# A mixture-of-experts gather: every fourth up row of the first tile summed on VectorE instead of TensorE

## What is computed

```
# x_c: 128 tokens of the normalised stream; 8 heads, top 16 experts of each
s1, s2 = queries . sub-keys;  v1, i1 = top_k(s1, 16);  v2, i2 = top_k(s2, 16)
top_s, pos = top_k(v1[:, None] + v2[None, :], 16);  eidx = i1 * 128 + i2 at pos
g = softmax(top_s)
a = gelu(x_c . expert_down[eidx])              # one number for each token and expert
y = sum over heads and experts of (g * a) * expert_up[eidx]
x = x + y;  out = rmsnorm(x)
```

## Time and profile before

| | |
|---|---|
| median of 3 runs | 1003.92 us (1002.21 to 1005.22) |
| profiled execution | 1000.79 us, span 999.0 us |
| mean granted TensorE clock | 0.938 of full speed |
| first gather issued | 312.15 us from the span's start |
| first dot of tile 0, of tile 1 | 319.87 us, 666.38 us |
| last dot | 988.66 us |
| busy: TensorE, VectorE, ScalarE, GpSimd | 847.4, 563.1, 416.7, 244.0 us |
| moved by the gathers | 268.45 MB, 65.9% of what 16 DMA engines can take in the span |

### The profile page before, as it was taken

One profiled execution on the slowest core, in us unless ns is written; L12 is line 12 of the kernel. 1 busy time (PEld: TensorE's weight loads), 2 busy tenths in 40 slices (PEclk: granted clock), 3 DMA queues, 4 the chain that ended last, 5 costly groups with the idle time before them and its releaser, 6 DMA issues.

```text
span 999.0 us, 9382 instructions
## 1 busy us (share of the span) xinstructions
PE 847.4 (85%) x3163; PEld 478.0 (48%) x3163; DVE 563.1 (56%) x1336; ACT 416.7 (42%) x1082; POOL 244.0 (24%) x267
## 2 busy tenths in 40 slices
PE   5999999999797988988879999887686877877876
PEld 4999986647745635533334355432232322322322
DVE  5544432112225757477686675758668587685743
ACT  5434434213302454356643543435354344343533
POOL 0000000000002332333333423333333333434330
PEclk9999995585998999999999999999999999999999
DMA  9869652000016998999999999999999999999995
GB/s 335 289 144 382 225 212 63 22 0 1 1 41 266 367 406 311 372 423 423 420 415 403 364 423 366 360 423 378 420 421 422 421 420 422 409 407 418 416 422 237
DMA packets 63299, 316.33 MB, mean 317 GB/s; under 512 B 7891, under 2 KB 10004, under 8 KB 30484
## 3 DMA queue, kind: packets, MB, share of 16 engines
q0 software_dynamic: 36864, 268.45, 65.9%
q1 hardware_dynamic: 26340, 47.28, 14.1%
q10 hardware_dynamic: 48, 0.01, 0.0%
HBM read 313.10 MB, written 2.62 MB: 316 GB/s over the span
## 4 chain that ended last, share of the span: by engine, by line
PE 48%; DMA 27%; DVE 15%; ACT 7%; issue 2%; POOL 0%; POOLq 0%; DVEq 0%; ACTq 0%
DMA qkvb<-in_expert_rows,expert_idx 20%; PE y L1152 10%; PE a_bank L964 8%; DMA spare<-in_expert_rows,expert_idx 7%; PE v_bank L1152 7%; PE a_bank L957 6%; PE v_bank L957 6%; DVE qkvb L890 5%; PE v_bank L964 4%; PE v_bank L1043 2%; PE y L1064 2%; DVE spare L890 2%; PE v_bank L1047 1%; ACT diag L617 1%; DVE key_idx L828 1%
## 5 line engine op out<-in xcount | busy, mean ns | idle before, releaser
L462 POOL DMA_INDIRECT qkvb<-in_expert_rows,expert_idx x172 | 162.1, 943 | 592.3 <-DVE expert_idx L866 309.7
L1152 PE MATMUL v_bank<-qkvb,diag 128*128 128x512 f32 x344 | 169.4, 627 | 48.7 <-ACT diag L617 48.7
L610 ACT ACTIVATE gelu<-dots 128x1 f32<-128x1 f32 x256 | 51.6, 202 | 347.6 <-DVE dots L890 347.2
L1152 PE MATMUL y<-qkvb,diag 128*128 128x512 f32 x344 | 166.1, 626 | 35.8 <-ACT diag L617 35.7
L890 DVE CUSTOM_DVE_ANT_0 qkvb<-h_psum,qkvb 128x1024 f32<-128x1024 f32 x86 | 104.2, 1223 | 75.0 <-DMA qkvb<-in_expert_rows,expert_idx 74.8
L890 DVE CUSTOM_DVE_ANT_0 qkvb<-a_bank,qkvb 128x1024 f32<-128x1024 f32 x86 | 104.2, 1223 | 69.6 <-DMA qkvb<-in_expert_rows,expert_idx 68.9
L1152 PEld LDWEIGHTS v_bank<-qkvb,diag 128*128 128x128 f32 x344 | 61.8, 193 | 155.7 <-ACT diag L617 103.2
L1152 PEld LDWEIGHTS y<-qkvb,diag 128*128 128x128 f32 x344 | 64.7, 197 | 126.3 <-issue 63.1
L462 POOL DMA_INDIRECT spare<-in_expert_rows,expert_idx x84 | 80.3, 956 | 142.0 <-PE y L1152 74.2
L617 ACT ACTIVATE diag<-ident,wgt 128x128 f32<-128x128 f32 x256 | 102.7, 401 | 8.3
L1152 PE MATMUL v_bank<-spare,diag 128*128 128x512 f32 x168 | 84.2, 634 | 22.3 <-ACT diag L617 22.3
(11 more groups left out here) (194 smaller groups left out, 1163.1 us busy)
## 6 DMA issues: line engine op xcount, KB each, us to landing
weights<-in_w_in SPq DMA_DIRECT2D x6, 2048.0 KB, 18.5
weights<-in_w_xk SPq DMA_DIRECT2D x2, 2048.0 KB, 12.7
weights<-in_w_xv SPq DMA_DIRECT2D x2, 2048.0 KB, 15.5
weights<-in_w_out SPq DMA_DIRECT2D x2, 2048.0 KB, 18.3
weights<-in_w_xq SPq DMA_DIRECT2D x2, 2048.0 KB, 8.0
weights<-in_w_xo SPq DMA_DIRECT2D x2, 2048.0 KB, 8.2
weights<-in_w_peer_query SPq DMA_DIRECT2D x2, 2048.0 KB, 7.9
qkvb<-in_expert_rows,expert_idx POOLq DMA_INDIRECT x172
```

The lines of the kernel that those rows point to most:

```text
L462: pool.indirect_dma_start(ROWS[n % NS], None, expert_rows, bass.IndirectOffsetOnAxis(ap=IDX[:, H % 3, k:k + 1], axis=0))\
L610: nc.scalar.activation(gel[:, i:i + 1], dots[:, i:i + 1], ACT.Gelu).then_inc(gelu_done, 1)
L1152: ins = nc.tensor.matmul(YP[t][:, b * BLK:(b + 1) * BLK], diag[:, i, :], ROWS[i][:, D + b * BLK:D + (b + 1) * BLK], start=False, stop=n % ...
```

## The change

Slots of tile 0 with n % 4 == 3, up to slot 123, become side slots. For them ScalarE makes the weight but no diagonal, and TensorE makes no `up`. VectorE multiplies the up half with the weight (one scalar for each partition) and sums it in a new SBUF tile `y_side`. It does so three slots later: `side(n)` stands directly behind `dot(n + 3)`, ahead of the steps of `slots` and of the top-k work. Each increments a new semaphore `side_used`. GpSimd, when it gathers slot n + 6 into the buffer of a side slot n, waits for `side_used` and not for `up_used`. After slot 127 TensorE adds `y_side` to the sum of tile 0 with two identity products (`add_side`), and `root_y` of tile 0 waits for these (`y_full`). Room for `y_side` (4 KB in each partition) is found by laying the 32 gain rows, read early, in a part of `probs_t`. Tile 1 is not changed. The diff, shortened:

```diff
+SIDE_EVERY, SIDE_LAG = 4, 3
...
+    def on_side(n):
+        return n < SPT - SIDE_LAG and n % SIDE_EVERY == SIDE_EVERY - 1
+    def sides(n):
+        return sum(on_side(m) for m in range(n))
+    def mains(n):
+        return n - sides(n)
...
-        grow = sb("gain_rows", [32, P])
+        grow = PT[0:32, 0, 0:P]
+        YSIDE = sb("y_side", [P, D])
...
-                if n >= NS:
-                    pool.wait_ge(up_used, n - NS + 1)
+                if n >= NS and on_side(n - NS):
+                    pool.wait_ge(side_used, sides(n - NS + 1))
+                elif n >= NS:
+                    pool.wait_ge(up_used, mains(n - NS + 1))
...
-                act.wait_ge(w_done, n + 1)
-                nc.scalar.activation(diag[:, i, :], ident[:, :], ACT.Copy, scale=wgt[:, i:i + 1])\
-                    .then_inc(diag_done, 1)
+                if not on_side(n):
+                    act.wait_ge(w_done, n + 1)
+                    nc.scalar.activation(diag[:, i, :], ident[:, :], ACT.Copy, scale=wgt[:, i:i + 1])\
+                        .then_inc(diag_done, 1)
...
-                    act.wait_ge(up_used, SPT)
+                    act.wait_ge(y_full, 1)
...
+            def side(n):
+                i = n % NS
+                dve.wait_ge(w_done, n + 1)
+                rows, w = ROWS[i][:, D:2 * D], wgt[:, i:i + 1]
+                if sides(n) == 0:
+                    ins = nc.vector.tensor_scalar(YSIDE[:, :], rows, w, None, ALU.mult)
+                else:
+                    dve.wait_ge(side_used, sides(n))
+                    ins = nc.vector.scalar_tensor_tensor(out=YSIDE[:, :], in0=rows, scalar=w, in1=YSIDE[:, :],
+                                                         op0=ALU.mult, op1=ALU.add)
+                ins.then_inc(side_used, 1)
...
                 dot(n)
+                if n >= SIDE_LAG and on_side(n - SIDE_LAG):
+                    side(n - SIDE_LAG)
...
+            def add_side():
+                pe.wait_ge(side_used, sides(SPT))
+                for b in range(2):
+                    ins = nc.tensor.matmul(YP[0][:, b * BLK:(b + 1) * BLK], ident[:, :],
+                                           YSIDE[:, b * BLK:(b + 1) * BLK], start=False, stop=True)
+                ins.then_inc(y_full, 1)
...
-                up(n)
+                if not on_side(n):
+                    up(n)
+                if n == SPT - 1:
+                    add_side()
```

More of the change, by code:

```diff
@@ L343, in hybrid_layer @@
                                                    sem("up_used"))
+        side_used, y_full = sem("side_used"), sem("y_full")
         dve_ch = sem("dve_ch")
@@ L629, in _ @@
                 if n == SPT + NB:
-                    act.wait_ge(up_used, SPT)
+                    act.wait_ge(y_full, 1)
                     root(("root_y", 0, 0), YP[0][:, :], HTpage[0], D)
             nc.scalar.activation(stat[:, 15:16], eps[:, 0:1], ACT.Sqrt)
-            act.wait_ge(up_used, T * SPT)
+            act.wait_ge(up_used, mains(T * SPT))
             root(("root_y", 1, 0), YP[1][:, :], HTpage[1], D)
@@ L1145, in y_start @@
                                      start=True, stop=False)
+            def add_side():
[4 more added lines that the diff above has]
+                ins.then_inc(y_full, 1)
             def up(n):
                 i, t = n % NS, n // SPT
-                pe.wait_ge(diag_done, n + 1)
+                pe.wait_ge(diag_done, mains(n + 1))
                 for b in range(2):
@@ L1153, in up @@
                                            ROWS[i][:, D + b * BLK:D + (b + 1) * BLK], start=False,
-                                           stop=n % SPT == SPT - 1)
+                                           stop=t > 0 and n % SPT == SPT - 1)
                 ins.then_inc(up_used, 1)
```

## The result

The changed kernel takes 1036.16 us (median of 4 runs, 1030.29 to 1038.35) against 1003.07 us (4 runs) of the kernel before. The ratio is 1.032, with a 95% interval of 1.0272 to 1.0368: 3.2% slower.

A forecast was written before the change was run, and what follows sets the result against it. Expert-row gathers were taken to bound tile 1 and nearly tile 0. 31 cycles of 11.5 us plus 6 us of additions gave 362.5 against 334.3 us, +28.2 us on 1000.8, and with 3.1 us more 1032 us (1006 to 1056).

The forecast's parts named there:

- The release step: Side slot's buffer in tile 0: dot 1.15, side operation 1.28, GpSimd start 0.2, together 2.65 us from dot(n+3).
- The gather's floor: No expert-row gather lands sooner than 5.4 us after issue, while 4.81 us are left before use.
- the queue must run dry at every side slot: DMA gather queue, tile 0: slot n+6's row cannot land in the 4.81 us left after the late release.
- rival (b): Gather lands in time, side release never binds, 20 of 25.9 us dry DMA time recovered: 984 us; chance 0.07.
- The second row: Burst after a late release: 8.85 us from first issue to use of the second gathered row, range 8.69 to 9.17.
- The cycle: Four slots of tile 0 from one late release to the next: 11.5 us against 9.95 gather-bound, 31 times, 356.5 us.
- the additions: Added to the 31 cycles: 3 us for top-k work on VectorE, 3 us for TensorE's blocks; sum 362.5 us.
- TensorE's blocks: Seven large matmul steps in the slots, such as 7.31 us after slot 21; their gaps make nearly all dry time.
- VectorE has room: VectorE in tile 0 takes about 39 us more on 234.55 of 346 us busy, reaching 79%.
- Rival (d): VectorE's side operation also stretches GpSimd's issues by 0.91 us at each of 31 slots: 1060 us; chance 0.08.
- Most of the prize is indeed taken, but inside a longer cycle: Tile 0: most of the 25.9 us of dry DMA queue is recovered, yet four slots take 11.5 us against 9.95.
- gaps of 8 us behind TensorE's blocks are gone: Sign in the profile after: GpSimd's long issue gaps in tile 0 behind the large matmul steps disappear.

The follow-up runs named there:

- load_release: Kernel before plus a dummy VectorE operation at the 31 side places, GpSimd waiting for it as well before reusing a side slot's buffer; 1037.46 us, ratio 1.0342.
- relief_only: Changed kernel with the side slots' part of the sum left out: no TensorE up, no VectorE operation, buffers released early; ratio 0.997 to the kernel before.
- load_only: Kernel before plus a dummy VectorE operation of the same form at the 31 side places, TensorE making all ups and releases; 1007.08 us, ratio 1.0046.
- lag 2: Changed kernel with side(n) directly behind dot(n+2), not dot(n+3); 1011.91 us, ratio 1.0083 to the kernel before.
- lag 1: Changed kernel with side(n) directly behind dot(n+1), not dot(n+3); 1006.94 us, ratio 1.005 to the kernel before.

## Why the prediction was right

The forecast was 1032 us (1006 to 1056), slower; 1036.16 was measured. Step by step:

- The release step: 2.65 us from dot(n+3) to the issue; 2.70 in the median of the 31 cycles. 28 of the 31 show as waits for VectorE's new line, where I said 31.
- Two readings in that step were wrong, without changing it. The time to landing is recorded for 24 of the 145 gathers only, all in one buffer, so "over 145 gathers" says too much; but of all 256 no slot was used less than 5.44 us behind its issue, and load_release, whose trace has all 256 landings, shows 5.3 us as the least. And the other gather in flight landed by 414.30, which is 2.36 us behind slot 34's issue, not ahead of its landing.
- The gather's floor: 5.4 us; in the changed kernel slot n+6 is used 5.64 us behind its issue in the median, 5.47 at least. The step "the queue must run dry at every side slot" is right, and rival (b) falls: even with the relief free of all cost, 333.1 us, there was no gain of 20 us. Its price was wrong for another reason than the one I weighed (the floor): I put 20 of 25.9 us as recoverable by a lighter TensorE, and relief_only recovers 1.2. The 53.3 us that TensorE was to lose are 15.8 us of busy time on the page (847.4 to 831.6), because its products were slower in the mean (see the last section).
- The second row: 8.85 us from the first issue taken, 8.99 in the median.
- The cycle: 11.5 us taken, 11.73 in the median; with the additions 362.5 us for the stretch against 367.0. The cycles vary from 10.77 to 13.42 us. The 4.5 us that the sum is short lie in the two small additions, not in the cycle: the 21 cycles that neither addition touches have a mean of 11.50 us. The seven from dot(2) to dot(6) of a head's slots, with the top-k work, add 5.8 us to that where I put 3. Three others, from dot(26), dot(90) and dot(110), take 13.42, 12.74 and 13.10 us and add 4.8 us where I put 3 for TensorE's blocks. The first two are those of the steps after slots 21 and 85. In the third the issue of slot 113 comes 1.77 us behind the end of side(107), where 0.27 is usual, and the trace names nothing that held it. That the 21 cycles meet 11.5 us so closely is partly luck: 8.85 us was a pick between 8.69 and 9.17, from three bursts.
- VectorE has room: 2.8 us for its load (ratio 1.0046). I had put nothing; it is small.
- Rival (d) asked for stretched issues at all 31 slots; there was one at a side operation. The reason given, that GpSimd waits for that very operation, fits: where it doesn't (load_only), six of 1.6 us or more appear beside the new operation.
- "Most of the prize is indeed taken, but inside a longer cycle" was loose, and so was "gaps of 8 us behind TensorE's blocks are gone". GpSimd still stands 7.92, 6.80 and 5.75 us for TensorE before slots 8, 28 and 92; before slots 34, 86, 106 and 116 it has shrunk to 0.3 to 2.1 us. But it would have stood still anyway: relief under a late release gives 3.2 us by two lengths, which the times can't tell from nothing.

## What to carry to other kernels

Moving work off a busy engine moves the release of its buffers too. Write down when the last reader of each buffer comes, in the old place and in the new, and hold it against the time that the ring of buffers leaves (buffers x period - release): here 4.8 us were left (6 x 2.487 - 10.1) where the shortest transfer took 5.4. That is the least that is needed, not enough: with lag 2 some 7.3 us were left by the same sum, and the slots still took 3.3 us more than with lag 1. Part of that can be that its side operations ended 8.2 us behind dot(n) in the median, where the sum has 7.6 to the release; no run shows the rest. Take the lag in time, not in slots: beside other work on the engine one slot of lag was 4.7 us. If what an engine delays is a queue that issues in order, look for the releases that come last and mend those, or deepen the queue; lightening the mean did next to nothing here.

## What the runs showed of the hardware

- When GpSimd began an indirect DMA while a `scalar_tensor_tensor` with two operands in SBUF was running on VectorE, the issue ended 0.81 us behind the end of that operation: 19 issues of load_only were stretched so, from 0.94 us to 0.98 to 1.82, the operation itself kept its 1.28 us. Where the operation began while an issue was under way (seven times there), nothing was stretched. Where the issue began within 0.06 us of the operation's start (slots 59 and 75), the issue kept its 0.94 us and the operation took 1.31.
- TensorE's granted clock in the slots of tile 0, a mean of stretches at full and at half speed, fell from 0.97 to 0.87 in the changed kernel, and was 0.90 in relief_only. In load_release, with the same late release but all its products, it was 0.95 (320 to 666 us), so most of the fall comes with the relief. The products with a diagonal weight took 592 ns in the median before and after; in the mean they took 747 ns (qkvb, 320 to 665 us) against 626 before, because more of them ran at half speed: 75 of 348 in that stretch took over 1 us, 16 of 508 before. So a part of what is taken off TensorE comes back as slower products, while the 64-product step after slot 21 took 7.31 us before, in the change and in relief_only. No run tells what this costs.
- In the 31 cycles of the changed kernel the first slot behind a late release was used 5.64 us behind its issue in the median (5.47 to 7.41), and the next one 3.28 us behind it (2.46 to 3.91), though its issue was only 1.24 us later. Slots of the undisturbed gather come 2.49 us apart.
